# Fourteen bursts of row products in place of seventeen, woven into the eight head pairs of a hybrid decoder step

## The chip, the cores and the metric

The kernel runs on one core of a Trainium2 chip. The metric is device time in microseconds of one execution; lower is better. Before the change it is 2447.63 us, the median of 3 runs (2447.49 to 2448.1).

## What is computed

One inference step of a one-layer decoder, for a prompt of 256 rows and 8 samples of 8 rows (320 rows in all), in float32. Each row is projected; three branches (a RWKV-7 recurrence, a chunked spatial gating, a cross-attention to a memory) are each multiplied by a weight matrix, gated and summed, and a gated MLP follows. What matters here, cut from the reference:

```python
def step(S, inp):                      # per head, over the rows in time
    r_t, w_t, k_t, v_t, av_t, bv_t = inp
    sa = jnp.einsum('bhvk,bhk->bhv', S, av_t)
    S = S * w_t[:, :, None, :] + sa[..., None] * bv_t[:, :, None, :] + v_t[..., None] * k_t[:, :, None, :]
    return S, jnp.einsum('bhvk,bhk->bhv', S, r_t)
...
mu = jnp.mean(y, axis=-1, keepdims=True)
var = jnp.mean(jnp.square(y - mu), axis=-1, keepdims=True)
yn = ((y - mu) * lax.rsqrt(var + GN_EPS)).reshape(B, T, W) * lnx_w + lnx_b
...
br = jnp.einsum('btnw,nwd->btnd', branches, p['w_branch'])
gates = jax.nn.sigmoid(gt.reshape(B, T, N_BRANCH, D_MODEL))
mix = jnp.sum(gates * br, axis=2) @ p['w_out']
```

The recurrence has 16 heads of 64 channels. It is computed in chunks of 64 rows: within a chunk a triangular system is solved by products (an inverse built by repeated squaring), and a state is handed from chunk to chunk.

## The kernel before

The stage that the change touches is `wkv_pe`, `wkv_dve` and `wkv_act`: a loop over eight **head pairs** (two heads side by side in the 128 partitions). For each pair TensorE does two kinds of work. The first is the recurrence: 44 small groups of matmuls, named in the table `PR` in the order in which they run (`A`, `bonus`, `B`, ... `RT1`, `RT2`, `Q`, ... `Z3`, `X4`, `G`, `S0` to `S3`, `X`, `g`, `mean`, `trp`, `var`, `tr0`, `tr1`), most of them on 64x64 quarters of the array (line 1152). Nearly every group's result is copied or masked by VectorE before a later group can use it, and the results share a ring of three PSUM banks. The second kind is independent of the recurrence: the **row products** of the gate projections and of the branches that are finished (lines 248, 249 and 257: 320 columns each on the whole array, weights split in a high and a low part). Per pair they use 6 units of weights, 48 matmuls each, and `pe_group_steps` gives them out in **steps** of 6 matmuls, 8 steps to a unit.

The table `STEPS` says how many steps TensorE issues ahead of each group. `begin(name)` issues them first, and only then waits for the semaphores that the group needs:

```python
p = PR[name]
assert p == done[0], name
for _ in range(STEPS.get(p, 0) - (Y_STEPS if name == "g" else 0)):
    next(steps, None)
```

`Y_STEPS` (3) of the steps of `g` come ahead of the recurrence's output `y` in `bank[6]`, the rest ahead of the `g` group. A run of steps without another group between is called a burst here. There are 17 in a pair before: at `A`, `A2`, `RT1`, `RT2`, `Q`, `XB`, `Z2`, `Z3`, `S0`, `S1`, `S2`, `S3`, `X`, ahead of `y`, `g`, `mean` and `var`.

VectorE's order (`wkv_dve`) is written out by hand. Besides the copies of the recurrence it makes the low parts of the weights (`weights_low`, line 218), adds the finished branch tiles (`branch`, lines 1748 and 1752) and prepares the next pair's operands (`prepare_...`). After the copy of state `S2` (line 957) stand: `weights_low(3)`, the sample state, state `S3`, `branch(0, 1)`, the addition of `X`, `prepare_norm` with a reciprocal, `weights_low(4)`, `prepare_al`, the copy of `y` (line 976), `prepare_rest`, `branch(1, 0)`, the `g` gate (line 980), the subtraction of the mean (line 983) and its square, on which `var` (line 1285) waits. ScalarE's order depends on `STEPS` too: `UNIT_END` gives the group at which each unit of row products is complete, and ScalarE converts the high part of unit j + 2 (`branch_act_unit`) ahead of the first of its own copies whose group stands behind `UNIT_END[j]`.

Of the kernel before, what the change touches and what calls it, by code (L numbers as in the profile page):

```python
# [108 lines left out]
def hybrid_step(nc, A, O):  # L109
    ctx = ExitStack()  # L110
    with ctx:
# [731 lines left out]
        def wkv_start_dve(dve, vv, beside):  # L843
# [23 lines left out]
            for t in range(4):  # L867
# [2 lines left out]

        STEPS = {"A": 8, "A2": 3, "RT1": 3, "RT2": 3, "Q": 3, "XB": 3, "Z2": 4, "Z3": 4, "S0": 2, "S1": 2, "S2": 2, "S3": 1, "X": 2,
                 "g": 5, "mean": 2, "var": 1}
        Y_STEPS = 3
        STEPS = {PR[_n]: v for _n, v in STEPS.items()}
        assert sum(STEPS.values()) == 48, sum(STEPS.values())
        UNIT_END = [next(p for p in range(NPR) if sum(STEPS.get(x, 0) for x in range(p + 1)) >= 8 * (j + 1)) for j in range(6)]

# [217 lines left out]
        def wkv_pe(pe, n):  # L1097
            u, t = U_BR[n], T_BR[n]
            for i in range(4 * n, 4 * n + 4):
# [18 lines left out]
                def begin(name, *needs):  # L1118
# [5 lines that stand above are left out]
# [1376 lines left out]
```

How the kernel before makes its waits and increments, by code:

```python
    def do(self, ins, name=None):  # L84
        name = name or self.own
        ins.then_inc(self.sem(name), 1)
        self.n[name] = self.n.get(name, 0) + 1
        self.eng.wait_ge(self.sem(name), self.value(name))
# [97 lines left out]
        def load_unit(sp, src, c, k=0, i=0):  # L188
            if c >= 2 or k:
                count = lin(c - 1, k, i)
                if k:
                    count = sp.to_reg(count)
                    sp.wait_ge(S("hi_done"), 1)
                sp.wait_ge(S("hi_done"), count)
                sp.wait_ge(S("lo_done"), count)
            sp.dma_start(raw[c % 2][:, :].rearrange("p (k n) -> p k n", n=src.shape[2]), src)\
              .then_inc(S(f"raw_loaded{c % 2}"), 16)
# [1 line left out]
        def pe_left(eng, c, k, i, parts_k):  # L201
            if c >= NS or k:
                eng.wait_ge(S("parts"), lin(parts_of(c - NS), parts_k, i))
# [1 line left out]
        def hi_unit(act, c, k=0, i=0, pk=None):  # L206
            if c >= U_END:
                return
            act.wait_ge(S(f"raw_loaded{c % 2}"), lin(16 * (c // 2 + 1), 8 * k, i))
            pe_left(act, c, k, i, 2 * k if pk is None else pk)
            act.activation(hi[c % NS][:, :], raw[c % 2][:, :], ACT.Copy).then_inc(S("hi_done"), 1)
# [1 line left out]
        def lo_unit(dve, c, k=0, i=0, pk=None):  # L213
            if c >= U_END:
                return
            dve.wait_ge(S("hi_done"), lin(c + 1, k, i))
            pe_left(dve, c, k, i, 2 * k if pk is None else pk)
            dve.tensor_tensor(lo[c % NS][:, :], raw[c % 2][:, :], hi[c % NS][:, :], ALU.subtract)\
```

## Time and profile before

| | before |
|---|---|
| median of 3 runs | 2447.63 us |
| profiled execution, its own time | 2445.91 us |
| its span on the core | 2444.2 us |
| TensorE busy | 2392.5 us (98%) |
| VectorE busy | 1467.3 us (60%) |
| ScalarE busy | 893.4 us (37%) |
| GpSimd busy | 121.0 us (5%) |
| granted TensorE clock, mean | 0.995 |
| one head pair (second of eight), from its first row product to the next pair's | 631.62 to 707.96 us |

The profiled execution took 1.72 us more than its span, and 1.72 us less than the median of the runs. Busy shares are means over stages with different limits, so a stage has to be read from its own rows. In a timeline, a gap in square brackets is the idle time of the engine ahead of the row, with what released it.

### The profile page before, as it was taken

The page shows a single profiled execution, that of the slowest core. Times are in us where ns is not written, and L with a number is a line of the kernel's source. Part 1 is how long each engine was busy: PE and PEld are TensorE (multiplying, and loading weights), DVE is VectorE, ACT ScalarE, POOL GpSimd, SP SyncE. Part 2 cuts the span into 40 slices and gives each one's busy share as a digit, 9 for nine tenths or more (in the row PEclk, how much of TensorE's full clock was granted, in tenths as well). Part 3 has the DMA queues.
Part 4 walks back from the last instruction along what each step waited for, and adds up shares of the span by engine and source line. Part 5 has one row for each costly group of instructions (what it writes and reads, how often), then busy time and mean ns, then how long its engine had stood idle before and what let it go on. Part 6 is the DMA issues. An engine that isn't in the chain of part 4 may idle for free.

```text
span 2444.2 us, 48594 instructions
## 1 busy us (share of the span) xinstructions
PE 2392.5 (98%) x19598; PEld 2273.3 (93%) x19598; DVE 1467.3 (60%) x2060; ACT 893.4 (37%) x1038; POOL 121.0 (5%) x195
## 2 busy tenths in 40 slices
PE   8999999999999999999999998999999999999998
PEld 6799888899888888888999987999999999999998
DVE  5545544565677666776545446666665666666676
ACT  6343344343333233332434333333333333333334
POOL 2000010100000010000000001000000000000003
PEclk9999999999999999999999998999999999999999
DMA  7554376343332243322444632444444444444443
GB/s 261 175 167 143 127 282 243 126 135 97 99 94 81 94 140 99 94 80 93 143 154 145 205 120 86 143 151 149 149 148 150 149 147 154 137 154 154 150 143 109
DMA packets 282189, 346.67 MB, mean 142 GB/s; under 512 B 6957, under 2 KB 240733, under 8 KB 280907
## 3 DMA queue, kind: packets, MB, share of 16 engines
q1 hardware_dynamic: 272315, 308.44, 38.7%
q0 software_dynamic: 9712, 36.30, 4.5%
q8 instruction: 104, 1.70, 0.3%
q14 instruction: 26, 0.21, 0.0%
q10 hardware_dynamic: 32, 0.01, 0.0%
HBM read 333.83 MB, written 10.89 MB: 141 GB/s over the span
## 4 chain that ended last, share of the span: by engine, by line
PE 86%; DVE 8%; issue 3%; DMA 1%; ACT 1%; DVEq 0%; SPq 0%; POOL 0%; ACTq 0%
PE bank L248 20%; PE bank L257 20%; PE bank L249 19%; PE bank L227 5%; PE bank L228 5%; PE bank L229 5%; PE bank L1152 5%; DVE work L893 1%; ACT hi L211 1%; DVE lo L218 1%; PE bank L1168 1%; DVE q L820 1%; PE bank L477 1%; PE bank L1626 1%; DMA raw<-in_w_out 0%
## 5 line engine op out<-in xcount | busy, mean ns | idle before, releaser
L248 PE MATMUL bank<-ah,hi 128*128 128x320 f32 x3232 | 970.9, 314 | 7.8 <-DVE al L1943 7.2
L218 DVE TENSOR_TENSOR lo<-raw,hi 128x2048 fp32r<-128x2048 f32 x286 | 655.8, 2293 | 519.5 <-ACT hi L211 503.1
L249 PE MATMUL bank<-al,hi 128*128 128x320 f32 x3232 | 957.5, 310 | 0.0
L211 ACT ACTIVATE hi<-raw 128x2048 fp32r<-128x2048 f32 x286 | 547.9, 1916 | 943.7 <-PE bank L257 691.7
L248 PEld LDWEIGHTS bank<-ah,hi 128*128 128x128 f32 x3232 | 608.7, 188 | 24.4 <-issue 18.2
L249 PEld LDWEIGHTS bank<-al,hi 128*128 128x128 f32 x3232 | 609.2, 188 | 0.3
L257 PE MATMUL bank<-ah,lo 128*128 128x320 f32 x3232 | 554.3, 312 | 0.0
L257 PEld LDWEIGHTS bank<-ah,lo 128*128 128x128 f32 x3232 | 492.3, 188 | 5.1 <-issue 1.6
L227 PE MATMUL bank<-bh,hi 128*128 128x320 f32 x704 | 219.0, 311 | 0.2 <-DVE work L2214 0.2
L228 PE MATMUL bank<-bl,hi 128*128 128x320 f32 x704 | 217.9, 309 | 0.0
L229 PE MATMUL bank<-bh,lo 128*128 128x320 f32 x704 | 217.8, 309 | 0.0
L1152 PE MATMUL bank<-work 64*64 64x64 f32 (+2 forms) x3680 | 166.0, 236 | 5.4 <-DVE work L893 4.3
L1152 PEld LDWEIGHTS bank<-work 64*64 64x64 f32 x3680 | 134.1, 134 | 35.7 <-issue 24.6
L227 PEld LDWEIGHTS bank<-bh,hi 128*128 128x128 f32 x704 | 132.2, 188 | 0.6 <-issue 0.6
L228 PEld LDWEIGHTS bank<-bl,hi 128*128 128x128 f32 x704 | 132.3, 188 | 0.0
L229 PEld LDWEIGHTS bank<-bh,lo 128*128 128x128 f32 x704 | 132.2, 188 | 0.0
L2214 DVE TENSOR_TENSOR work<-work,bank 128x320 f32<-128x320 f32 x176 | 85.6, 486 | 56.4 <-PE bank L229 45.7
L248 PE MATMUL bank<-bh,hi 128*128 128x320 f32 x384 | 118.1, 321 | 0.0
L249 PE MATMUL bank<-bl,hi 128*128 128x320 f32 x384 | 113.6, 309 | 0.0
L2188 DVE SCALAR_TENSOR_TENSOR rw<-rw,prm 128x336 f32<-128x336 f32 x176 | 100.2, 569 | 22.2 <-DVE rw L2186 1.4
L893 DVE TENSOR_TENSOR work<-work,bank 128x512 f32<-128x512 f32 (+3 forms) x56 | 28.9, 517 | 97.4 <-PE bank L1152 95.4
L248 PEld LDWEIGHTS bank<-bh,hi 128*128 128x128 f32 x384 | 72.1, 188 | 2.3
(361 smaller groups left out, 2000.8 us busy)
## 6 DMA issues: line engine op xcount, KB each, us to landing
raw<-in_w_in SPq DMA_DIRECT2D x98, 1024.0 KB, 5.2
raw<-in_w_up SPq DMA_DIRECT2D x88, 1024.0 KB, 5.1
raw<-in_w_down SPq DMA_DIRECT2D x44, 1024.0 KB, 5.1
raw<-in_w_branch SPq DMA_DIRECT2D x24, 1024.0 KB, 5.4
raw<-in_w_out SPq DMA_DIRECT2D x16, 1024.0 KB, 5.5
raw<-in_w_mem_k SPq DMA_DIRECT2D x8, 1024.0 KB, 5.6
raw<-in_w_mem_v SPq DMA_DIRECT2D x8, 1024.0 KB, 5.2
work<-in_cache_mem_k POOLq DMA_DIRECT2D x8, 1024.0 KB, 6.3
```

What stands on the lines that cost most here:

```text
L211: act.activation(hi[c % NS][:, :], raw[c % 2][:, :], ACT.Copy).then_inc(S("hi_done"), 1)
L218: dve.tensor_tensor(lo[c % NS][:, :], raw[c % 2][:, :], hi[c % NS][:, :], ALU.subtract)\
L227: pe.matmul(out, a_hi, b_hi, start=first, stop=False)
L228: pe.matmul(out, a_hi, b_lo, start=False, stop=False)
L229: return pe.matmul(out, a_lo, b_hi, start=False, stop=last)
L248: pe.matmul(out, w, xh[:, 8 * h + k, :], start=h + k == 0, stop=False)
L249: pe.matmul(out, w, xl[:, 8 * h + k, :], start=False, stop=False)
L257: last = pe.matmul(out, w, xh[:, 8 * h + k, :], start=False, stop=h == units - 1 and k == 7)
L893: vv.do(dve.tensor_tensor(o, a, b, op), sem)
L1152: last = pe.matmul(out[r, :], a[r, :], b[r, :], start=start and m == 0, stop=stop and m == len(pairs) - 1, **kw)
L2188: vv.do(dve.scalar_tensor_tensor(out=o, in0=x, scalar=w, in1=o, op0=ALU.mult, op1=ALU.add), "gate_conv" if j == 2 and q % 8 == 3 else None)
L2214: dve.tensor_tensor(f, f, bank[b][:, 0:T], ALU.add).then_inc(S(f"tile_out{b}"), 1)
```

## The change

Only the table `STEPS` is changed. The number of steps in a pair stays 48.

```diff
-        STEPS = {"A": 8, "A2": 3, "RT1": 3, "RT2": 3, "Q": 3, "XB": 3, "Z2": 4, "Z3": 4, "S0": 2, "S1": 2, "S2": 2, "S3": 1, "X": 2,
-                 "g": 5, "mean": 2, "var": 1}
+        STEPS = {"A": 8, "A2": 4, "RT1": 4, "RT2": 4, "Q": 3, "XB": 3, "Z2": 4, "Z3": 3, "S0": 2, "S1": 2, "S2": 2, "X": 3,
+                 "g": 5, "mean": 1}
```

`A2`, `RT1` and `RT2` get one step more each, `X` one more, `Z3` and `mean` one less, and the single steps of `S3` and `var` are gone: 14 bursts.

On TensorE, around the last states (64x512 is `S4`; the two rows of 64x64 behind it are `S3`), before:

```order
L1152 MATMUL bank<-work 64x512 x4
L248 MATMUL bank<-ah,hi 128x320
L249 MATMUL bank<-al,hi 128x320
L248 MATMUL bank<-ah,hi 128x320
L249 MATMUL bank<-al,hi 128x320
L248 MATMUL bank<-ah,hi 128x320
L249 MATMUL bank<-al,hi 128x320
L1152 MATMUL bank<-work 64x64 x4
L1152 MATMUL bank<-q,work 64x64 x2
```

and in the changed kernel:

```order
L1152 MATMUL bank<-work 64x512 x4
L1152 MATMUL bank<-work 64x64 x4
L1152 MATMUL bank<-q,work 64x64 x2
L257 MATMUL bank<-ah,lo 128x320 x6
L248 MATMUL bank<-bh,hi 128x320
L249 MATMUL bank<-bl,hi 128x320
```

The six row products between `S4` and `S3` are gone from there; the burst behind `S3` (ahead of `X`) is of 18 matmuls in place of 12.

On TensorE, at the end of a pair (line 1273 is `mean`, 1282 `trp`, 1285 `var`, 1278 `tr0` and `tr1`), as a difference from before to the changed kernel:

```order
-L248 MATMUL bank<-bh,hi 128x320
-L249 MATMUL bank<-bl,hi 128x320
-L257 MATMUL bank<-bh,lo 128x320 x2
 L1273 MATMUL bank<-work,head_ones 128x320
 L1282 MATMUL bank<-ident,q 64x128
-L257 MATMUL bank<-bh,lo 128x320 x6
 L1285 MATMUL bank<-work,head_ones 128x320
 L1278 MATMUL bank<-ident,work 64x128 x8
```

The step ahead of `var` is gone, and of the two ahead of `mean` one is left; what they held has been issued earlier.

On ScalarE, behind the gate activations of unit 1 (line 1739, the first row), as a difference from before to the changed kernel; 128x320 of line 1021 is the copy of `kaT`, 128x512 that of `s0t`, 128x192 that of `alT`, and line 211 the conversion of unit 2:

```order
 L1739 ACTIVATE small<-bank 128x320
 L1070 REGISTER_ALU
+L1021 ACTIVATE work<-bank 128x320
+L90 REGISTER_ALU
+L1070 REGISTER_ALU
 L1021 ACTIVATE q<-bank 128x512
 L90 REGISTER_ALU
+L209 REGISTER_ALU
+L204 REGISTER_ALU
+L211 ACTIVATE hi<-raw 128x2048
 L1070 REGISTER_ALU
 L1021 ACTIVATE work<-bank 128x192
```

The copy of `kaT`, which stood ahead of the conversion and the gate activations of unit 1, now stands behind them, and the conversion of unit 2, which stood behind the copy of `alT`, now stands ahead of it. The orders of VectorE, SyncE and GpSimd are the same in both kernels.

## Rows read from the trace of the kernel before

**Rows 1.** The page: span, and the chain that ended last.
```profile
span 2444.2 us, 48594 instructions
...
PE 86%; DVE 8%; issue 3%; DMA 1%; ACT 1%; DVEq 0%; SPq 0%; POOL 0%; ACTq 0%
```

**Rows 2.** Windows: busy us of each engine by stretch; PEclk is granted clock.
```profile
631.62:688.98 57.36, 56.66 (x759) 52.14 (x758) 34.95 (x55) 19.54 (x23) 5.14 (x9) 1.00 0.29 87
688.98:706.55 17.57, 17.13 (x187) 14.19 (x184) 15.42 (x23) 5.20 (x5) 0.00 (x0) 1.00 0.39 121
706.55:707.96 1.41, 1.40 (x10) 1.18 (x11) 1.07 (x3) 0.05 (x1) 0.00 (x0) 1.00 0.00 0
...
918.26:936.21 17.95, 17.13 (x187) 14.19 (x184) 15.42 (x23) 5.25 (x5) 0.00 (x0) 1.00 0.37 118
```

**Rows 3.** Timeline of TensorE, bursts at `A` and `A2`: start us, us, instruction.
```profile
631.62 0.39 PE L248 MATMUL bank<-ah,hi 128*128 128x320 f32 x1
...
638.84 0.80 PE L1152 MATMUL bank<-work 64*64 64x64 f32 x20
...
642.45 0.42 PE L248 MATMUL bank<-ah,hi 128*128 128x320 f32 x1
...
645.28 0.62 PE L1152 MATMUL bank<-work 64*64 64x64 f32 x14
```

**Rows 4.** Timeline of VectorE, the addition of `RT2`.
```profile
656.75 0.49 DVE L893 TENSOR_TENSOR work<-work,bank 128x320 f32<-128x320 f32 x1 [3.60 <-PE bank L1152]
```

**Rows 5.** Timeline of VectorE from `Z3` to `G`, then TensorE at `S0`.
```profile
679.78 0.69 DVE L893 TENSOR_TENSOR work<-work,bank 128x512 f32<-128x512 f32 x1 [2.54 <-PE bank L1152]
...
683.17 0.36 DVE L893 TENSOR_TENSOR work<-bank,m_id 128x192 f32<-128x192 f32 x1
...
683.58 0.45 PE L1152 MATMUL bank<-work 64*64 64x64 f32 x8 [0.54 <-DVE work L893]
```

**Rows 6.** Timeline of VectorE from the copy of `S2` to the square.
```profile
688.98 0.28 DVE L957 TENSOR_SCALAR q<-bank,q 128x64 f32<-128x64 f32 x1 [0.65 <-PE bank L1152]
...
701.57 0.49 DVE L976 COPY work<-bank 128x320 f32<-128x320 f32 x1
...
704.72 0.55 DVE L980 SCALAR_TENSOR_TENSOR work<-work,prm,bank 128x320 f32<-128x320 f32 x1 [0.25 <-DVE mix L1752]
...
705.92 0.49 DVE L893 TENSOR_TENSOR work<-work 128x320 f32<-128x320 f32 x1
```

**Rows 7.** Timeline of TensorE from `g` to `var`.
```profile
702.12 0.81 PE L1271 MATMUL bank<-q 128*128 128x320 f32 x2
...
704.51 0.70 PE L1273 MATMUL bank<-work,head_ones 128*128 128x320 f32 x2
...
705.08 1.12 PE L257 MATMUL bank<-bh,lo 128*128 128x320 f32 x6
706.56 0.78 PE L1285 MATMUL bank<-work,head_ones 128*128 128x320 f32 x2 [0.35 <-DVE work L893]
```

**Rows 8.** Timeline of TensorE, ends of groups: into a burst, into another group.
```profile
686.20 0.28 PE L1152 MATMUL bank<-q,work 64*64 64x64 f32 x4
686.41 1.15 PE L257 MATMUL bank<-ah,lo 128*128 128x320 f32 x6
...
688.65 0.28 PE L1152 MATMUL bank<-q,work 64*64 64x64 f32 x4
688.76 1.89 PE L1152 MATMUL bank<-work 64*64 64x512 f32 x8
```

**Rows 9.** Timeline of ScalarE, unit 1: conversion and gate activations.
```profile
655.13 1.91 ACT L211 ACTIVATE hi<-raw 128x2048 fp32r<-128x2048 f32 x1 [1.51 <-PE bank L257]
...
658.36 0.77 ACT L1739 ACTIVATE small<-bank 128x320 f32<-128x320 f32 x2
```

**Rows 10.** TensorE after the last branch: a gap; windows of what follows.
```profile
1457.66 0.95 PE L477 MATMUL bank<-ident,rw 128*128 128x128 f32 x3 [3.67 <-DVE mix L1937]
...
1457.50:1464.00 6.50, 6.34 (x16) 3.53 (x17) 4.89 (x11) 3.30 (x7) 5.10 (x6) 0.50 0.00 0
```

## The prediction

> **What bounds the kernel now.** I read the page first. TensorE is busy for 98% of the span, but the chain that ended last has VectorE in 8% of it [rows 1], so there are places where TensorE waits, and the question is which of them lie in the head pairs. The windows come next [rows 2]. They cut the second head pair (76.34 us) at two events: the copy of `S2` on VectorE (688.98) and the start of `var` on TensorE (706.55). Between these two VectorE is busy for 15.42 of 17.57 us, and in the part ahead of them for 34.95 of 57.36 us.
>
> The timelines then say who waits for whom. In the first part VectorE waits for TensorE: 3.60 us ahead of the addition of `RT2` [rows 4] and 2.54 us ahead of that of `Z3` [rows 5]. There TensorE sets the pace, with one exception, 0.54 us at `S0`, where it waits for VectorE's copy of `G` [rows 5]. In the second part it is the other way round. VectorE gets `S2` after 0.65 us of waiting, and from there works down its list to the square at 705.92. The small gaps that remain, such as the 0.25 us ahead of line 980, are released by VectorE itself [rows 6]. TensorE starts `g` at 702.12, right behind the copy of `y` (701.57 plus 0.49), and `var` at 706.56, right behind the square (705.92 plus 0.49), after an idle 0.35 us [rows 6, 7]. So the stretch from the copy of `S2` to `var`, 17.57 us, is as long as VectorE's list, and TensorE's row products only fill it. In the fifth pair it is 17.95 us, with the same 15.42 us of VectorE work [rows 2].
>
> A pair is therefore a sum of two terms: a first part whose length is TensorE's work, and a second part whose length is VectorE's.
>
> **What a step and a burst cost.** The burst at `A` has 48 matmuls and takes 638.84 - 631.62 = 7.22 us; that at `A2` has 18 and takes 645.28 - 642.45 = 2.83 us [rows 3]. The difference, 4.39 us over 30 matmuls, is 0.146 us each, so a step of 6 costs 0.878 us. What is left of the short burst, 2.83 - 18 x 0.1463 = 0.20 us, is paid once per burst. Ahead of it the group's last four matmuls take 686.41 - 686.20 = 0.21 us into a burst, and 688.76 - 688.65 = 0.11 us into another group [rows 8]. A burst between two quartered groups thus costs 0.30 us beside its steps.
>
> The Trainium skill (TensorEngine Tiling, Key Properties) says that changing the tiling mode drains TensorE. The 0.30 us agree with it, and by this rule alone three bursts fewer in each of eight pairs would be a gain of 24 x 0.30 = 7.2 us; by the rows of this trace the sum is the one below, since all three bursts that go lie where TensorE waits for VectorE.
>
> **The change, part by part**, for one pair.
>
> - `A2`, `RT1` and `RT2`: plus one step each, all in the first part, where TensorE sets the pace and nothing on it waits. The longer bursts give VectorE more time for copies for which it already waited for TensorE (3.60 us at `RT2`), so they hide nothing. Plus 3 x 0.878 = 2.63 us.
> - `Z3`: minus one step, also in the first part. `Z3` then comes 0.878 us earlier. VectorE had waited 2.54 us for it, so it is still free in time, and `G`, the logs and the 0.54 us at `S0` all move forward together. Minus 0.88 us.
> - `S3`: minus one step and one burst, in the second part. `S3` has to wait for the copy of `S2` (done at 689.26), and `S4`, which runs from 688.76 for 1.89 us, covers that. VectorE comes to the copy of `S3` only behind `weights_low(3)` and the sample state. `X` gets the step back, so the `X` group starts within 0.3 us of where it did. The stretch up to the `g` group holds 8 steps in both kernels; what TensorE saves in the change of mode becomes waiting for the copy of `y`. Zero.
> - `mean`: minus one step, and `var`: minus its only step, both between `g` and `var`. `g` starts at 702.12 as before, since the copy of `y` releases it. `mean` starts at about 704.51 - 0.88 = 703.63, `trp` half a microsecond later, and then TensorE has nothing until the square is done at 706.41. VectorE's list between the two is unchanged. The 1.76 us of row products that covered this wait are now elsewhere, and the wait at `var` grows from 0.35 us to some 2.1 us. Zero for the stretch, and this is why the steps added in the first part are not paid back.
> - ScalarE: the copy of `kaT` now stands behind the conversion of unit 1 and its gate activations, 1.91 us, a table load and 0.77 us, in all 659.13 - 655.13 = 4.0 us [rows 9]. They can start when the `RT1` burst ends; the copy is first wanted at `Q`, behind the group of `RT1`, the `RT2` burst (24 matmuls, 3.7 us), its group and the `Q` burst (2.8 us), 6.5 us of row products alone against 4.0. If that cover were gone, `Q` would wait and pay what is missing. Zero. The conversion of unit 2 ahead of `alT` is taken before the `XB` burst's last two steps are out, zero too.
> - The units of weights: no unit is wanted before its conversion. The tightest is unit 5, whose low part (`weights_low(3)`, right behind the copy of `S2`) is first wanted at step 43. That is now the first step ahead of `y` and was the third; it still stands behind the whole burst and group of `X`, so the conversion has more than 3 us. If it were late, TensorE would wait inside VectorE's stretch and lose nothing until some 2 us.
>
> **Sum.** The first part grows by 3 - 1 = 2 steps, 1.76 us: 57.36 to 59.12 us. The second stays at 17.57. Over eight pairs that is 8 x 1.76 = 14.0 us. Against the profiled execution's own time, 2445.91 + 14.0 = 2459.95 us; the median of the runs lies 1.72 us above that execution, so 2461.7 us. Small things take a little off (`mean`, coming earlier, may take back a part of the 0.38 us by which the fifth pair's stretch is longer), and I say 2461.4. Its own range is 2457.5 to 2465: two steps per pair are known to about 0.02 us each, and the rest allows 0.5 us per pair for waits at either end of VectorE's stretch.
>
> **The rivals.**
>
> - **Faster, through fewer changes of mode.** If TensorE set the pace everywhere, the steps would only change places and 24 bursts would save 7.2 us: 2440.4 us. For it speaks that TensorE is 98% busy. It decides where VectorE's stretch is shorter than TensorE's work in it. That work is now 17.57 - 0.35 = 17.2 us at most, and after the change about 17.2 - 1.76 - 0.6 = 14.8 us, so VectorE's list would have to be under 14.8 us. Its busy time alone is 15.42 us [rows 2]. Chance 0.03.
> - **No measurable change.** Part of VectorE's stretch would have to follow TensorE: if `S4`, `X` and `mean` coming earlier let VectorE be done 1.2 us sooner, 9.6 of the 14 us would be given back, and the time would be 2452 us, within 4.9 us of before. The gaps in its list are released by itself, which speaks against this. Chance 0.04.
> - **Slower still, by the clock.** The granted clock was 1.00 in the pairs [rows 2]. After a gap of 3.67 us with little work ahead of it, a stretch of 6.5 us was granted 0.50, that is 1.2 GHz [rows 10]. The new wait of 2.1 us in each pair is shorter. If it did the same, 6.5 us at half the clock would hold half as much TensorE work, 3.3 us lost per pair, 26 us in all: 2488 us. The Trainium skill (TensorE: Matmul & The Clock Gate, Part 1) says that activity is what releases the throttle; by that rule an idle gap is the danger, and the fall here agrees. Chance 0.03.
>
> **How the numbers follow.** The likeliest case has 0.90. The range that leaves out no more than 2 in 10 is that case's own, 2457.5 to 2465. A measurement of this kernel tells 0.2%, 4.9 us, from no change. The likeliest case and the clock lie above it: slower 0.93, same 0.04, faster 0.03.
>
> **What the changed kernel's profile would show.** Right: a pair of some 78.1 us; the part up to the copy of `S2` longer by 1.76 us; the stretch from that copy to `var` still 17.6 us, with less TensorE work and an idle gap of about 2.1 us ahead of `var`, released by line 893 on VectorE; bursts at `A2`, `RT1` and `RT2` of 3.7 us with VectorE waiting longer behind each; the wait at `S0` still about 0.5 us. Wrong: a `var` stretch under 16.5 us would mean that VectorE had been following TensorE after all; a wait at `RT1`, `Q` or `Z3` would mean that a copy or a conversion had been late; a granted clock under 1.00 in the pairs would be the third rival.

## The result

| | before | changed kernel |
|---|---|---|
| median | 2447.63 us (2444.86 to 2451.51, 5 runs) | 2463.68 us (2459.92 to 2467.14, 5 runs) |
| ratio of the times | | 1.0065, 95% interval 1.0049 to 1.008 |
| profiled execution, its own time | 2445.91 us | 2459.92 us |
| its span | 2444.2 us | 2458.2 us |
| granted TensorE clock, mean | 0.995 | 0.994 |

The change makes the kernel slower by 0.65%, 16 us by the medians and 14.0 us by the two profiled executions. 2461.4 us had been forecast, with a range of 2457.5 to 2465.

The texts ahead of the result count 14 bursts in a pair of the changed kernel; there are 15. `mean` keeps one of its two steps, so only the bursts of `S3` and `var` are gone, and TensorE's timeline of the second pair shows 15 runs of row products. The change takes away two bursts in a pair, 16 in all.

### The profile page after: what moved, and what is told of

It reads as the page before. It is cut to its first block, busy times and chain, and to the rows that moved or that the text cites. A ratio compares the mean times of both kernels' runs of the same rounds, so it can differ in the third digit from the quotient of the medians.

```text
span 2458.2 us, 48594 instructions
## 1 busy us (share of the span) xinstructions
PE 2389.4 (97%) x19598; PEld 2273.6 (92%) x19598; DVE 1467.4 (60%) x2060; ACT 893.7 (36%) x1038; POOL 121.4 (5%) x195
## 4 chain that ended last, share of the span: by engine, by line
PE 87%; DVE 8%; issue 3%; ACT 1%; DMA 1%; DVEq 0%; SPq 0%; ACTq 0%
PE bank L248 20%; PE bank L257 20%; PE bank L249 20%; PE bank L227 5%; PE bank L229 5%; PE bank L228 5%; PE bank L1152 5%; DVE work L893 1%; ACT hi L211 1%; PE bank L1168 1%; DVE q L820 1%; DVE lo L218 1%; PE bank L477 1%; PE bank L1626 1%; PE bank L1968 0%
## 5 line engine op out<-in xcount | busy, mean ns | idle before, releaser
L257 PE MATMUL bank<-ah,lo 128*128 128x320 f32 x3232 | 548.8, 310 | 0.0
```

The lines of the kernel that those rows point to most:

```text
L257: last = pe.matmul(out, w, xh[:, 8 * h + k, :], start=False, stop=h == units - 1 and k == 7)
```

## The profile after

The windows of the changed kernel, the same stretches as in [rows 2] (from the pair's first row product to the copy of `S2`, on to `var`, on to the next pair), and a fourth behind the `var` of the fourth pair. The columns are span of the stretch, then busy us of TensorE, its weight loads, VectorE, ScalarE and GpSimd, then the granted clock, the DMA share and GB/s.

```profile
633.59:692.79 59.20, 58.49 (x772) 53.98 (x771) 35.03 (x55) 19.54 (x23) 5.15 (x9) 1.00 0.27 84
692.79:710.37 17.58, 15.03 (x175) 12.49 (x172) 15.42 (x23) 5.25 (x5) 0.00 (x0) 1.00 0.38 121
710.37:711.69 1.32, 1.32 (x9) 1.08 (x10) 0.99 (x3) 0.00 (x0) 0.00 (x0) 1.00 0.00 0
866.57:869.98 3.41, 3.41 (x13) 2.57 (x14) 2.80 (x6) 1.43 (x2) 0.00 (x0) 0.52 0.00 0
```

The stretch up to `var` is what it was, 17.58 us against 17.57, with the same 15.42 us of VectorE work. TensorE is busy in it for 15.03 us in place of 17.13: two steps (1.76 us) and 0.34 us for the bursts. The part ahead of it has grown from 57.36 to 59.20 us. (The border between the last and the first stretch moved by 0.09 us, since the last product of `tr1` is seen a little differently; from `var` to the copy of `S2` it is 60.52 us against 58.76.)

The timeline of TensorE from `g` to the next pair, to be held against [rows 7]:

```profile
705.93 0.81 PE L1271 MATMUL bank<-q 128*128 128x320 f32 x2 [0.44 <-DVE work L976]
706.33 1.28 PE L257 MATMUL bank<-bh,lo 128*128 128x320 f32 x6
707.45 0.70 PE L1273 MATMUL bank<-work,head_ones 128*128 128x320 f32 x2
707.99 0.27 PE L1282 MATMUL bank<-ident,q 128*64 128x128 f32 x1
710.37 0.78 PE L1285 MATMUL bank<-work,head_ones 128*128 128x320 f32 x2 [2.11 <-DVE work L893]
```

One step stands ahead of `mean` (line 257, 6 matmuls) and none ahead of `var`. The wait at `var` is 2.11 us where it was 0.35, and `g` now waits 0.44 us for the copy of `y`. VectorE, in the same places as in [rows 4], [rows 5] and [rows 6]:

```profile
661.45 0.49 DVE L893 TENSOR_TENSOR work<-work,bank 128x320 f32<-128x320 f32 x1 [4.48 <-PE bank L1152]
...
683.59 0.69 DVE L893 TENSOR_TENSOR work<-work,bank 128x512 f32<-128x512 f32 x1 [1.66 <-PE bank L1152]
...
692.79 0.28 DVE L957 TENSOR_SCALAR q<-bank,q 128x64 f32<-128x64 f32 x1 [0.65 <-PE bank L1152]
...
709.73 0.49 DVE L893 TENSOR_TENSOR work<-work 128x320 f32<-128x320 f32 x1
```

At `RT2` VectorE waits 4.48 us in place of 3.60: the longer burst has only made it wait longer. At `Z3` it waits 0.88 us less, one step. TensorE's only wait that the timeline shows between `var` and the copy of `S2` is still that at `S0`, 0.54 us:

```profile
687.39 0.45 PE L1152 MATMUL bank<-work 64*64 64x64 f32 x8 [0.54 <-DVE work L893]
```

## Experiments

In each, the pair that is measured runs from one `var` to the next, in the second pair unless said otherwise: 76.34 us before, 78.10 us in the changed kernel.

**The step of `S3` given to `X`, alone.**

```diff
-        "S3": 1, "X": 2,
+        "X": 3,
```

> One part of the change alone: the single step of S3 goes to X (S3 0, X 3), all else as before: 16 bursts. Theory A (the stretch from the copy of S2 to var is as long as VectorE's list): the pair stays 76.3 us, that stretch 17.6 us, and the 0.30 us saved in the change of tiling mode turn into waiting for the copy of y; time as before, 0 +- 0.1%. Rival B (a burst fewer is a gain wherever it is): 8 x 0.30 = 2.4 us faster, pair 76.0 us. Rival C (S3 without cover waits for the copy of S2): slower, up to 0.9 us a pair, 7 us.

Measured: 2451.65 us against 2449.38 for before in the same session, ratio 1.0004 (0.9994 to 1.0013). Its windows, up to the copy of `S2` and on to `var`, and TensorE's `g`:

```profile
632.66:690.08 57.42, 56.72 (x759) 52.19 (x759) 35.00 (x56) 19.55 (x23) 5.13 (x9) 1.00 0.29 87
690.08:707.63 17.55, 16.78 (x187) 14.26 (x184) 15.39 (x23) 5.20 (x5) 0.00 (x0) 1.00 0.39 121
...
703.20 0.81 PE L1271 MATMUL bank<-q 128*128 128x320 f32 x2 [0.43 <-DVE work L976]
```

A burst fewer, and the stretch is as long as before. TensorE has 0.35 us less to do in it (16.78 against 17.13), and about the same third of a microsecond now stands as a wait at `g`, where [rows 7] show none. Rivals B and C are out: B would have been 2.4 us faster, and the interval ends at 1.5 us faster. This part of the change costs nothing and gives nothing.

**The steps of `mean` and `var` given to `RT1` and `RT2`, alone.**

```diff
-        "A2": 3, "RT1": 3, "RT2": 3, ... "mean": 2, "var": 1
+        "A2": 3, "RT1": 4, "RT2": 4, ... "mean": 1
```

> The other part alone: mean 1 and var 0, and their two steps to RT1 and RT2 (4 each); S3, X, A2 and Z3 as before. Theory A: the whole cost is here. First part 57.4 + 1.76 = 59.1 us, stretch from the copy of S2 to var still 17.6 us, pair 78.1 us, wait at var 2.1 us; 14 us slower plus 1.7 us for each wait at var after which the clock falls. Rival B (fewer bursts gain): 2 us faster. Rival D (the cost comes from the steps taken from Z3 and S3 or from the order of ScalarE's copy of kaT, which stays as before here): no change.

Measured: 2463.64 us against 2449.38, ratio 1.0057 (1.0043 to 1.0071). The windows from one copy of `S2` to `var` and on to the next copy of `S2`, and TensorE at `var`; then the windows of two stretches at half the clock, the first ahead of the head pairs, the second behind the `var` at 638.74:

```profile
700.64:718.21 17.57, 15.37 (x176) 12.42 (x172) 15.41 (x23) 5.25 (x5) 0.00 (x0) 1.00 0.38 121
718.21:778.72 60.51, 59.81 (x778) 55.05 (x780) 36.00 (x57) 19.66 (x23) 5.13 (x9) 1.00 0.27 82
...
718.21 0.78 PE L1285 MATMUL bank<-work,head_ones 128*128 128x320 f32 x2 [2.12 <-DVE work L893]
...
273.89:287.54 13.65, 13.65 (x43) 10.56 (x44) 3.76 (x4) 1.91 (x1) 0.00 (x0) 0.50 0.25 95
639.12:642.53 3.41, 3.41 (x15) 2.80 (x14) 2.96 (x6) 2.00 (x2) 0.00 (x0) 0.50 0.00 0
```

The pair is 78.08 us from copy to copy, as long as in the changed kernel, and the wait is the same too. It lies around the second `var`, since behind the first (638.74) the clock had fallen: from that `var` to the next it is 79.47 us. Behind the third `var` (796.28) it fell again, at 796.13 for 3.4 us. The whole cost of the steps lies in this part: rival D is out with its ScalarE order too, since the copy of `kaT` stands where it stood before here. (The conversion of unit 2 stands ahead of `alT` in this run as in the changed kernel; TensorE shows no wait for it.)

**One step more in the direction of the change.**

```diff
-        "A2": 4, "RT1": 4, "RT2": 4, ... "mean": 1
+        "A2": 5, "RT1": 4, "RT2": 4, ...
```

> The change and one step more in its direction: the last step of mean too goes to A2 (A2 5, RT1 4, RT2 4, Z3 3, X 3, mean 0, var 0), so nothing stands between g and var but mean and trp. Theory A: pair 78.10 + 0.88 = 78.98 us, wait at var about 2.8 us, 21 us slower than before by the steps alone. Theory E (the clock falls after such waits, once in eight in the profile of the changed kernel, at 1.7 us each): a longer wait makes it fall more often; three or more of the eight waits, 5 us or more on top of the 21. Without E the granted clock in the pairs stays 1.00 or falls in one of them, as after the change.

Measured: 2480.0 us against 2449.38, ratio 1.0125 (1.0111 to 1.014). In the first pair, where the clock held, from `var` to `var` 61.40 + 17.56 = 78.96 us, the 78.98 that theory A gives. The windows of that pair, then one behind the wait of 2.98 us in the third, and TensorE at that wait:

```profile
634.56:695.96 61.40, 60.70 (x784) 55.97 (x786) 36.01 (x57) 18.25 (x23) 5.13 (x9) 1.00 0.27 81
695.96:713.52 17.56, 14.15 (x169) 11.62 (x166) 15.40 (x23) 6.76 (x6) 0.00 (x0) 1.00 0.39 121
...
793.79:799.00 5.21, 5.21 (x19) 4.41 (x20) 4.20 (x9) 2.12 (x4) 0.80 (x2) 0.50 0.00 0
...
793.79 1.41 PE L1285 MATMUL bank<-work,head_ones 128*128 128x320 f32 x2 [2.98 <-DVE work L893]
```

A half-clock stretch begins at or near `var` in seven of the eight pairs; only the first is spared. A pair with one is 80.3 to 81.7 us long. The steps alone make 8 x 2.63 = 21 us, and the median is 31 us over before. Theory E holds. In the profile the seven pairs from the first `var` to the eighth take 29.8 us more than before (565.24 against 535.43), 11.4 us more than seven times 2.63, and six of them stand behind a fall.

**The opposite of the change: the waits covered.**

```diff
-        "RT1": 3, "RT2": 3, ... "S0": 2, ... "var": 1
+        "RT1": 2, "RT2": 2, ... "S0": 3, ... "var": 2
```

> The opposite of the change: a step from RT2 to S0 (2 and 3) and one from RT1 to var (2 and 2); 17 bursts. Theory A: TensorE's wait of 0.54 us at S0 and of 0.35 us at var are filled with row products, since VectorE had slack of 1.07 us at RT1 and 3.60 us at RT2: first part 57.36 - 1.76 + 0.34 = 55.9 us, second part 17.57 + 0.53 = 18.1 us, pair 76.34 - 0.89 = 75.45 us, 8 x 0.89 = 7 us faster. If the shorter bursts at RT1 and RT2 uncover a wait, less, down to no gain. Rival B (only the number of bursts counts): no change.

Measured: 2436.22 us against 2449.38, ratio 0.9954 (0.9941 to 0.9968), the lowest median of all the kernels run. The windows from `var` to the copy of `S2` and on to `var`; VectorE at `RT1` and `RT2`; TensorE at `S0` and at `var`, both without a wait:

```profile
629.62:686.56 56.94, 56.78 (x762) 52.20 (x762) 35.73 (x56) 19.66 (x23) 5.14 (x9) 1.00 0.30 87
686.56:704.49 17.93, 17.85 (x194) 15.14 (x190) 15.69 (x24) 5.25 (x5) 0.00 (x0) 1.00 0.40 119
...
649.63 0.49 DVE L893 TENSOR_TENSOR work<-work,bank 128x320 f32<-128x320 f32 x1 [0.18 <-PE bank L1152]
...
654.07 0.49 DVE L893 TENSOR_TENSOR work<-work,bank 128x320 f32<-128x320 f32 x1 [2.72 <-PE bank L1152]
...
681.16 0.45 PE L1152 MATMUL bank<-work 64*64 64x64 f32 x8
...
704.49 0.70 PE L1285 MATMUL bank<-work,head_ones 128*128 128x320 f32 x2
```

The pair is 74.87 us, 1.47 us shorter, where 0.89 had been expected. One step less in the first part and the wait at `S0` gone (0.54 us) give 0.88 + 0.6, and the second part grows by 0.36 only, since the step ahead of `var` also takes up what had been its wait. About 0.25 us more came at the groups between the bursts at `A` and `A2`. That TensorE had waited there for VectorE's mask of `A` is argued from the order, since the rows show no gap of TensorE there. VectorE's slack at `RT1` is used up but for 0.18 us.

**VectorE's list shortened, in the changed kernel.** The reciprocal of the key norms is left out, and a memset to 0.1 stands in its place, so the outputs that depend on the keys are others.

```diff
-            vv.do(dve.reciprocal(sq, sq))
+            vv.do(dve.memset(sq, 0.1))
```

> The changed kernel with VectorE's list shortened: the reciprocal of prepare_norm (2.15 us, between the copy of S2 and var) is left out, a memset of the same tile to 0.1 stands in its place, so the keys are not normalised. If VectorE's list sets the stretch from the copy of S2 to var (theory A), it falls from 17.6 us by what the list loses, some 1.85 us, to 15.7; the wait at var falls from 2.1 to 0.3 us, the pair from 78.1 to 76.25 us, 15 us faster than the changed kernel, about even with the kernel before, and the clock stays 1.00 in the pairs. If the row products added in the first part cost by themselves and VectorE's list does not matter (rival D), the pair stays above 77.5 us.

**The same edit in the kernel before.**

> The kernel before with the same reciprocal left out (a memset of 0.1 in its place, keys not normalised). Here TensorE's work fills the stretch but for 0.35 us at var, 0.15 us at g and some 0.25 us at beT, where it comes up to VectorE's list: theory A gives at most 0.75 us a pair, 6 us faster, against 15 us for the same edit in the changed kernel. If VectorE's list were not the pace, both would give the same.

Measured: 2448.75 us and 2443.54 us, against 2448.82 for before in the same session; ratios 1.0001 (0.9991 to 1.0011) and 0.9981 (0.997 to 0.9993). So the edit takes back the whole cost of the change in the one, and gives 5 us in the other. The stretch from the copy of `S2` to `var`, first in the changed kernel and then in that before:

```profile
693.55:709.41 15.86, 14.77 (x175) 12.49 (x172) 13.59 (x23) 5.06 (x5) 0.00 (x0) 1.00 0.44 134
```

```profile
695.31:712.39 17.08, 16.87 (x187) 14.19 (x184) 13.58 (x23) 5.06 (x5) 0.00 (x0) 1.00 0.40 125
```

In both VectorE's work falls by 1.83 us (15.42 to 13.59 and 13.58). In the changed kernel the stretch falls by 1.72 us, to 15.86; before the change only by 0.49, since TensorE's own work comes in the way. The pair is 76.37 us in the one and 75.85 in the other. This shows that the stretch runs at VectorE's pace, and that the row products taken out of it were hidden there. A wait of 1.1 us at `var` stays in the changed kernel, longer than the 0.3 expected: TensorE's own work there is 14.8 us.

**`branch(1, 0)` behind the square, in the changed kernel.**

```diff
                 prepare_rest(dve, vv, i + 1)
-                branch(1, 0)
...
                 tt(ysq, ym, ym, ALU.mult, "ym_sq")
+                branch(1, 0)
```

> The changed kernel with the two instructions of branch(1, 0) on VectorE (1.38 us of its list) moved from ahead of the g gate to behind the square, on which var waits. The simple form of theory A (only the list up to var counts): stretch 16.2 us, wait at var 0.75 us, pair 76.7 us, 11 us faster. But in the trace of before VectorE has no wait for TensorE from the copy of S2 through var and the next pair's weights up to the mask of A, and TensorE waits some 0.25 us at beT for that mask. If the list is one chain of 28 us to that mask (theory A2), the wait only moves: var 1.4 us sooner, beT waits 1.6 us, pair still 78.1 us.

Measured: 2460.59 us, ratio to before 1.005 (1.0033 to 1.0066). The windows from `var` to the copy of `S2` and on to `var`, TensorE behind that `var`, and VectorE at the subtraction of the mean ahead of it (line 982 here):

```profile
634.01:695.80 61.79, 60.13 (x778) 54.99 (x780) 36.98 (x59) 19.74 (x24) 5.13 (x9) 1.00 0.28 82
695.80:712.36 16.56, 15.03 (x175) 12.50 (x172) 14.45 (x22) 5.06 (x5) 0.00 (x0) 1.00 0.41 126
...
712.36 0.78 PE L1285 MATMUL bank<-work,head_ones 128*128 128x320 f32 x2 [1.09 <-DVE work L893]
...
714.01 0.63 PE L1278 MATMUL bank<-ident,work 128*64 128x128 f32 x4 [0.43 <-DVE q L988]
...
724.40 0.80 PE L1168 MATMUL bank<-m_id,work 64*64 64x64 f32 x20 [0.53 <-DVE work L893]
...
711.20 0.49 DVE L982 SCALAR_TENSOR_TENSOR work<-bank,work 128x320 f32<-128x320 f32 x1 [0.37 <-PE bank L1273]
```

The wait at `var` falls by 1.02 us and not by 1.38, since VectorE now comes to the subtraction too early and waits 0.37 us for `mean`. All of it comes back, as 0.43 us at `tr1` and 0.53 us at `beT`: the pair is 78.35 us, 0.25 us longer than in the changed kernel. Theory A2 holds. VectorE's list does not end at `var`; it runs on to the mask of `A` without waiting for TensorE longer than 0.2 us, and moving work inside it moves the wait. In this profile the clock stayed at 1.00 in the pairs, with waits of 1.1 us.

**The faster table with 16 bursts.**

```diff
-        "S3": 1, "X": 2, "g": 5, "mean": 2, "var": 2
+        "X": 3, "g": 5, "mean": 2, "var": 2
```

> The faster table of the run before (RT1 2, RT2 2, S0 3, var 2) and the step of S3 given to X (16 bursts). There TensorE works through the stretch from the copy of S2 to var (17.93 us against VectorE's 17.57), so the burst saved, 0.30 us, is now worth something: stretch 17.6 us, pair 74.87 - 0.3 = 74.6 us, 2 us faster than that run and 13 us faster than before. If VectorE's list is already the pace, nothing.

Measured: 2438.5 us against 2448.82, ratio 0.9954 (0.9937 to 0.9971), the same ratio as with 17 bursts. It missed: the stretch is 17.94 us, as with 17 bursts, and the 0.3 us saved stand as a wait at `g`:

```profile
700.51 0.81 PE L1271 MATMUL bank<-q 128*128 128x320 f32 x2 [0.43 <-DVE work L976]
```

The stretch has two parts. Up to the copy of `y` it goes at VectorE's pace even here, and only from `g` to `var` at TensorE's.

**The copy of `y` earlier, in that kernel.**

```diff
                 prepare_norm(dve, vv, i + 1)
-                weights_low(4)
                 prepare_al(dve, vv, i + 1)
...
                 prepare_rest(dve, vv, i + 1)
+                weights_low(4)
                 branch(1, 0)
```

> The table of the 16-burst run (RT1 2, RT2 2, S0 3, S3 0, X 3, var 2) and one edit of VectorE's order: weights_low(4), 2.29 us, moved from ahead of the copy of y to behind prepare_rest. In that run TensorE waited some 0.5 us at g for the copy of y although it set the pace from g to var. With the copy of y up to 2.3 us earlier this wait goes, and the stretch from the copy of S2 to var becomes TensorE's work, 17.94 - 0.48 = 17.5 us, or VectorE's whole list, 17.57, whichever is longer: pair 74.5 us, 3 us faster than the 16-burst run, 14 to 15 us faster than before. If the copy of y is not what held g, nothing.

Measured: 2437.99 us against 2446.74, ratio 0.997 (0.9957 to 0.9983). The wait at `g` is gone, but the stretch is 18.13 us and the pair 75.39, 0.5 us longer than without the edit. VectorE at the copy of `y` (line 975 here) and TensorE at `var`:

```profile
697.31 0.49 DVE L975 COPY work<-bank 128x320 f32<-128x320 f32 x1 [0.59 <-PE bank L1152]
...
704.58 0.51 PE L1285 MATMUL bank<-work,head_ones 128*128 128x320 f32 x1 [0.72 <-DVE work L893]
```

VectorE now comes to the copy of `y` before TensorE has it, waits 0.59 us there, and is late by 0.72 us at `var`. It is the same wait in the other direction.

**The changed kernel again.**

> The changed kernel once more, for the part of its time that its first profile leaves open: its span was 14.0 us over that of before, its median 16 us. If the waits of 2.1 us at var now and then bring the clock down (theory E; one in eight in the first profile), other executions show another number of them, one to three of the 24 half-clock microseconds fewer or more, with pairs of 78.1 us where none falls and 1.3 to 1.9 us more where one does, and the median stays 15 to 17 us over before. Without E all pairs are 78.1 to 78.3 us.

Measured: 2463.76 us against 2446.74, ratio 1.0072 (1.0059 to 1.0085), span of the profiled execution 2462.0 us. Two half-clock stretches begin at a `var`, the third and the eighth:

```profile
788.93:792.34 3.41, 3.41 (x13) 2.62 (x14) 2.80 (x6) 1.45 (x2) 0.00 (x0) 0.52 0.00 0
1181.59:1185.00 3.41, 3.32 (x12) 2.54 (x13) 2.60 (x6) 1.24 (x2) 0.00 (x0) 0.50 0.00 0
```

The pair behind the first is 79.47 us in place of 78.10; the other six are 78.07 to 78.58. So theory E holds here too: the number of falls differs from execution to execution. How much of the median's extra 2 us they make is not shown, since the clock falls elsewhere too. The profile of the kernel before without its reciprocal has a long stretch at half the clock ahead of the head pairs, as the run with `RT1` and `RT2` has:

```profile
274.53:288.18 13.65, 13.65 (x44) 10.57 (x43) 3.75 (x4) 1.91 (x1) 0.00 (x0) 0.50 0.25 88
```

The first `var` there comes at 636.54 us, against 630.22 in the profile of before, which has no fall at that place. The executions of before lie between 2444.85 and 2454.29 us in all, and its medians in three sessions were 2449.38, 2448.82 and 2446.74 us.

## Why the prediction was right, point by point

- **The two paces.** Right. The stretch from the copy of `S2` to `var` is 17.58 us in the changed kernel, and it became shorter only where VectorE's list ahead of `var` did (15.86, 17.08 and 16.56 us). The prediction let this list end at the square; it runs on to the mask of `A` in the next pair. The forecast did not need this, the experiment with `branch(1, 0)` did.
- **`A2`, `RT1`, `RT2`, `Z3`.** Right: two steps net, 1.76 us forecast, 60.52 - 58.76 = 1.76 us measured. VectorE's wait at `RT2` grew by a step (3.60 to 4.48 us), at `Z3` it fell by one (2.54 to 1.66).
- **`S3` and `X`: zero.** Right, and shown alone (ratio 1.0004). The 0.3 us of the mode change became a wait of 0.44 us at `g`.
- **`mean` and `var`: zero for the stretch, a wait of some 2.1 us.** Right: 2.11 us. That this part with its two steps is the whole cost was shown by making it alone. The 0.3 us taken off the sum because `mean` comes earlier did not come: in the fifth pair the stretch is 17.95 us after the change as before.

```profile
928.63:946.58 17.95, 15.03 (x176) 12.50 (x172) 15.41 (x23) 5.25 (x5) 0.00 (x0) 1.00 0.38 118
```

- **ScalarE and the units of weights: zero.** Right as far as seen: no new wait of TensorE stands in the first part of the second pair.
- **Fewer changes of mode as a gain.** The price of this rival was miscounted. Two bursts go in a pair and not three, so it should have been 16 x 0.30 = 4.8 us in place of 7.2; the forecast itself uses neither. The saving is real on TensorE for the burst at `S3`, 0.35 us less work in the run with `S3` alone. The Trainium skill (TensorEngine Tiling, Key Properties) says that a change of tiling mode drains TensorE, and these 0.35 us agree. The burst at `var` saved nothing beside its matmuls: with both gone TensorE's work fell by 2.10 us, of which 1.76 are the two steps. In no kernel here that took a burst out of VectorE's stretch was it worth any time.
- **The clock.** Here a size was off. The third rival, with a chance of 0.03, was priced as a fall in every pair, 3.3 us each, 26 us in all. Its sign, a granted clock under 1.00 in the pairs, was seen, but it came in part only: one of eight waits in the first profile of the changed kernel, two in the second. In the first, the stretch from `var` to the copy of `S2` behind the fall was 62.06 us against 60.52 in the pairs ahead of it; 0.28 us of that this pair had before the change too (59.04 against 58.76), so the fall cost 1.3 us. Eight times 1.76 is 14.1 us, with the fall 15.4, and `var` of the eighth pair came 15.6 us later than before (the first `var` was already 0.3 us later than its steps make it):

```profile
1165.65 0.78 PE L1285 MATMUL bank<-work,head_ones 128*128 128x320 f32 x2 [0.47 <-DVE work L893]
```

```profile
1181.27 0.78 PE L1285 MATMUL bank<-work,head_ones 128*128 128x320 f32 x2 [2.21 <-DVE work L893]
```

The first row is of the kernel before, the second of the changed one. The spans differ by 14.0 us only, so 1.6 us were given back behind the pairs. That the difference of the spans meets the 14.0 us of the sum so exactly is luck, since a fall and what was given back cancel in it. Part of what was given back lies at the half-clock stretches after the last branch [rows 10], which came 13.5 us later where the row products ahead of them came 15.1 us later, so less work fell into them; why the rest was given back was not followed. The median lies 2.3 us over the forecast. That falls behind `var` make this up is argued from the profiles, not counted in the executions that were only timed; falls ahead of the pairs, which kernels without the long waits have too, and the scatter of medians of the kernel before (2446.74 to 2449.38 us) are as large and were not separated from them.

## What to carry to other kernels

Filler work is free only where its engine waits for another, so the question for each place is who sets the pace there. Where the filler's own engine sets it, each step costs its full time (0.88 us here); where the other engine sets it, taking a step out only makes a wait. Read it from both sides: an engine with a gap released by the other has slack, an engine whose list runs without such gaps is the pace, and the two can change within one loop body (here more than once in 76 us). Put filler by the size of the wait, not by the count of bursts: two steps moved to where the waits of 0.54 and 0.35 us were gave 0.46%; two steps moved away from a wait cost 0.57%, with 16 bursts left, and in the change itself 0.65%, with 15.

## What the runs showed of the hardware

- At a wait of 2.1 to 2.5 us at `var`, in a stream of TensorE that is otherwise full, the granted clock fell to 0.5 (1.2 GHz) for 3.4 us in one, two and two of eight cases, in three profiles (two of the changed kernel, one of that with the steps at `RT1` and `RT2`); at a wait of 3.0 to 3.4 us in seven of eight, for 3.4 or 6.8 us. At waits of 0.35 and 1.1 us at `var` it never did. A fall at 2.1 us cost 1.3 to 1.4 us. The Trainium skill (TensorE: Matmul & The Clock Gate, Part 1) says that activity is what releases the throttle, and that the falls stand at idle gaps and come more often with the longer one agrees.
- The granted clock was 0.50 for 13.7 us ahead of the head pairs, at 274 to 288 us, in two profiles, and the timelines show no gap of TensorE in the 8 us before it fell; other profiles show 3.4 us at half the clock there, or none. So not every fall here stands at an idle gap, and the cause of these was not followed. With the 13.7 us the first `var` came some 6 us later (636.54 against 630.22, 638.74 against 632.27).
- A burst of whole-array row products between quartered groups cost 0.30 us beside its matmuls, 0.20 us in the burst and 0.10 us in the group ahead of it, in the pair read; taking one such burst away took 0.35 us off TensorE's work.
